# Gated products: the root-mean-square factors of four heads computed on four partitions and spread back by products

## The reference, cut to what matters

```python
def _hgrn_branch(q, v, f_fwd, f_bwd, og, norm_g, ...):
    ...
    o = (o_f + o_b[:, :, ::-1]).astype(jnp.float32)
    o = o * lax.rsqrt(jnp.mean(jnp.square(o), axis=-1, keepdims=True) + RMS_EPS)
    B, H, T, dh = o.shape
    o = (o.transpose(0, 2, 1, 3).reshape(B, T, H * dh) * norm_g).astype(q.dtype)
    return o * jax.nn.silu(og), s_f, s_b

def _merge(u_four, o_hgrn, gate_pre, w_fp, w_hp, w_o, b_o):
    g_four, g_hgrn = jnp.split(jax.nn.sigmoid(gate_pre...), N_BRANCHES, axis=-1)
    y = g_four * (_fourier_mix(u_four) @ w_fp) + g_hgrn * (o_hgrn @ w_hp)
    return y @ w_o + b_o
```

## Time and profile before

| | us |
|---|---|
| median of 3 runs | 3388.22 |
| lowest and highest | 3383.31, 3389.66 |
| span of the profiled execution | 3383.8 |
| of it, first to last instruction of the gated products | 1460.5 to 1726.8 |

### The profile page before, as it was taken

How to read it: one execution, slowest core, us unless ns; L and a number is a source line. 1 busy time by engine, 2 the same in 40 slices (tenths; PEclk the granted TensorE clock), 3 DMA queues, 4 the chain that set the end, 5 groups by cost and what they waited for, 6 DMA issues and landing times. The chain is left out here.

```text
span 3383.8 us, 35637 instructions
## 1 busy us (share of the span) xinstructions
PE 3140.5 (93%) x14552; PEld 2562.5 (76%) x14552; DVE 1852.5 (55%) x2585; ACT 615.2 (18%) x1048; POOL 301.3 (9%) x453
## 2 busy tenths in 40 slices
PE   5999999999996899929969999999999999999997
PEld 3878788888884688826758878888888778888886
DVE  3831133121222888657758775666655666666556
ACT  1421000111112556521001221111111101111110
POOL 0323011000001212200000000000000000000000
PEclk8999999999998999969989999999999999999999
DMA  6642233233235533345554721221114321111111
GB/s 216 208 138 78 75 101 124 103 122 115 96 107 165 150 109 111 99 158 193 173 172 148 226 77 48 63 69 63 56 48 126 122 69 58 58 60 60 50 44 62
DMA packets 261127, 365.32 MB, mean 108 GB/s; under 512 B 15443, under 2 KB 171363, under 8 KB 259430
## 3 DMA queue, kind: packets, MB, share of 16 engines
q1 hardware_dynamic: 203926, 197.33, 19.2%
q0 software_dynamic: 43680, 134.26, 11.4%
q10 hardware_dynamic: 13360, 31.46, 2.9%
HBM read 256.55 MB, written 106.44 MB: 107 GB/s over the span
## 5 line engine op out<-in xcount | busy, mean ns | idle before, releaser
L137 PE MATMUL head_bank<-head_hTh,head_wh 128*128 128x512 f32 x1024 | 407.2, 398 | 3.1 <-DVE head_hTl L549 2.3
L1971 PE MATMUL tail_bank<-tail_h2h,tail_w1h 128*128 128x512 f32 x1024 | 400.8, 391 | 4.5 <-DVE tail_w1l L1740 4.5
L139 PE MATMUL head_bank<-head_hTh,head_wl 128*128 128x512 f32 x1024 | 404.9, 395 | 0.0
L138 PE MATMUL head_bank<-head_hTl,head_wh 128*128 128x512 f32 x1024 | 404.9, 395 | 0.0
L1989 PE MATMUL tail_bank<-tail_w2h,tail_ah 128*128 128x512 f32 x1024 | 400.2, 391 | 4.0 <-DVE tail_acc L1770 4.0
L1972 PE MATMUL tail_bank<-tail_h2l,tail_w1h 128*128 128x512 f32 x1024 | 400.4, 391 | 0.0
L1973 PE MATMUL tail_bank<-tail_h2h,tail_w1l 128*128 128x512 f32 x1024 | 400.1, 391 | 0.0
L1990 PE MATMUL tail_bank<-tail_w2l,tail_ah 128*128 128x512 f32 x1024 | 399.8, 390 | 0.0
L1991 PE MATMUL tail_bank<-tail_w2h,tail_al 128*128 128x512 f32 x1024 | 399.8, 390 | 0.0
L557 DVE CAST head_wh<-head_raw 128x1024 fp32r<-128x1024 f32 x64 | 44.5, 695 | 583.5 <-PE head_bank L139 432.0
L1772 DVE TENSOR_TENSOR tail_acc<-tail_acc,tail_bank 128x512 f32<-128x512 f32 x416 | 275.6, 684 | 118.5 <-PE tail_bank L1991 116.4
(11 more groups left out here) (228 smaller groups left out, 4755.8 us busy)
## 6 DMA issues: line engine op xcount, KB each, us to landing
tail_raw<-in_w SPq DMA_DIRECT2D x128, 512.0 KB, 4.0
head_raw<-in_w_in SPq DMA_DIRECT2D x64, 512.0 KB, 4.1
scratch_proj<-head_stage POOLq DMA_DIRECT2D x128, 256.0 KB, 2.7
head_x<-in_w_ada ACTq DMA_DIRECT2D x8, 2048.0 KB, 10.1
merge_gates<-scratch_proj SPq DMA_DIRECT2D x32, 512.0 KB, 5.1
head_wa<-in_w_ada SPq DMA_DIRECT2D x8, 1024.0 KB, 5.3
mix_dec<-scratch_proj SPq DMA_DIRECT2D x32, 256.0 KB, 3.9
scratch_dft_a<-mix_fa POOLq DMA_DIRECT2D x32, 256.0 KB, 4.0
```

The costliest lines, as they stand in the source:

```text
L137: nc.tensor.matmul(out, wh, xh, start=(k == 0), stop=False)
L138: nc.tensor.matmul(out, wh, xl, start=False, stop=False)
L139: last = nc.tensor.matmul(out, wl, xh, start=False, stop=(k == k_tiles - 1))
L1971: nc.tensor.matmul(U[2 * e + c][:], w1h[:, e, k, :], hT[0][:, k, cs], start=(k == 0), stop=False)
```

## The change

The mean square is no longer spread over all partitions by its product. `sel[:, h, :]` is a weight tile of 128 x 4 whose column h is 1/128 and the rest zero; four products into the same bank, with `start` at the first and `stop` at the last, gather the four heads in rows 0 to 3 of one 4x512 tile. ScalarE takes one root of it (out `rr`), VectorE one reciprocal (`inverse`). Then `spread` multiplies `rr` with `back[:, h, :]`, a 4 x 128 tile that has ones in row h, and so puts head h's factor on all partitions of bank 7 (even h) or 6 (odd h). `part_c` multiplies straight from that bank.

The places in the queues change with it. VectorE: `inverse` in step 2, heads 0 and 1 in step 4, heads 2 and 3 in step 5, `part_d` in step 6. TensorE: heads 0 and 1 are spread after step 3, heads 2 and 3 after step 4; at the start the spreads stand behind the first and second `fourier` group.

```diff
+        sel, back = bx.sb("sel", [P, KB, KB]), bx.sb("back", [KB, KB, P])
+        rr = bx.sb("rr", [KB, 512])
+        sel_s, rc_s, br_s = bx.sem("sel_ready"), bx.sem("rms_inverse"), bx.sem("rms_spread")
...
+            def inverse(b):
+                dve.wait_ge(rt_s, b + 1)
+                if b:
+                    dve.wait_ge(br_s, KB * b)
+                nc.vector.reciprocal(rr[:], rr[:]).then_inc(rc_s, 1)
+
             def part_c(b, h):
 
-                dve.wait_ge(rt_s, KB * b + h + 1)
-                step.up(nc.vector.reciprocal(o2[:, 1, h], o2[:, 1, h]))
-                step.wait(dve)
-                nc.vector.scalar_tensor_tensor(sq[:, h], o2[:, 0, h], ng[:, h:h + 1], o2[:, 1, h], ALU.mult, ALU.mult
+                dve.wait_ge(br_s, KB * b + h + 1)
+                nc.vector.scalar_tensor_tensor(sq[:, h], o2[:, 0, h], ng[:, h:h + 1], bank[7 - h % 2][:], ALU.mult, ALU.mult
                                                ).then_inc(norm_s, 1)
...
+            step.up(nc.vector.memset(sel[:], 0.0))
+            step.wait(dve)
+            for h in range(KB):
+                nc.vector.memset(sel[:, h, h:h + 1], 1.0 / P)
+                last = nc.vector.tensor_copy(back[:, h, :], g["ident"][0:KB, h:h + 1].to_broadcast([KB, P]))
+            last.then_inc(sel_s, 1)
             part_a(0)
             weights(0, KB)
             part_b(0)
+            inverse(0)
...
-                    elif m < 5:
-                        for h in ((0, 1), (2,), (3,))[m - 2]:
+                    elif m == 2:
+                        inverse(b + 1)
+                    elif m in (4, 5):
+                        for h in ((0, 1), (2, 3))[m - 4]:
                             part_c(b + 1, h)
-                    elif m == 5:
+                    elif m == 6:
                         part_d(b + 1)
...
-                for h in range(KB):
-                    act.wait_ge(ms_s, KB * b + h + 1)
-                    nc.scalar.activation(o2[:, 1, h], bank[6 + h % 2][:], ACT.Sqrt, bias=g["eps"][:, 1:2]).then_inc(rt_s, 1)
+                act.wait_ge(ms_s, b + 1)
+                if b:
+                    act.wait_ge(br_s, KB * b)
+                nc.scalar.activation(rr[:], bank[6][0:KB, :], ACT.Sqrt, bias=g["eps"][0:KB, 1:2]).then_inc(rt_s, 1)
...
+                if b:
+                    pe.wait_ge(norm_s, KB * b)
+                else:
+                    pe.wait_ge(sel_s, 1)
                 pe.wait_ge(sq_s, b + 1)
                 for h in range(KB):
+                    last = nc.tensor.matmul(bank[6][0:KB, :], sel[:, h, :], sq[:, h], start=(h == 0), stop=(h == KB - 1))
+                last.then_inc(ms_s, 1)
+
+            def spread(b, heads):
+                for h in heads:
+                    pe.wait_ge(rc_s, b + 1)
                     if KB * b + h >= 2:
-                        pe.wait_ge(rt_s, KB * b + h - 1)
-                    nc.tensor.matmul(bank[6 + h % 2][:], g["mean"][:], sq[:, h], start=True, stop=True).then_inc(ms_s, 1)
+                        pe.wait_ge(norm_s, KB * b + h - 1)
+                    nc.tensor.matmul(bank[7 - h % 2][:], back[:, h, :], rr[:], start=True, stop=True).then_inc(br_s, 1)
...
             for m in range(3):
                 fourier(0, m)
+                if m < 2:
+                    spread(0, (2 * m, 2 * m + 1))
...
                     if m == 1 and b < NB - 1:
                         mean_square(b + 1)
+                    if m in (3, 4) and b < NB - 1:
+                        spread(b + 1, ((0, 1), (2, 3))[m - 3])
```

## The result

| | before | after |
|---|---|---|
| median of 4 runs, us | 3388.9 | 3419.1 |
| lowest and highest | 3383.3, 3390.3 | 3415.2, 3421.6 |
| span of the profiled execution | 3383.8 | 3413.3 |
| first sum-of-squares product to the end of block 3 | 251.6 | 281.0 |

The changed kernel is slower: ratio 1.0093, 95% interval 1.008 to 1.0106, some 30 us. The prediction had the sign; its 3400.5 us was 18.6 short, and the result lies above its range. The spans differ by 29.5 us and the stage by 29.4, so all of it is in the gated products.

A forecast was written before the change was run, and what follows sets the result against it. TensorE was taken to set the pace, waiting for VectorE at hand-overs. 6.3 us per hand-over, three times 18.9, minus 2.5 and 4.1 gave +12.3: span 3396.1, plus 4.4 to the median, 3400.5 us; range 3393 to 3413.

The forecast's parts named there:

- Reciprocal: VectorE, each block: one 4x512 reciprocal takes 3.34 us like each of the four wide ones, so VectorE loses 10.0 us.
- Selector products: TensorE's queue: four new spreading products per block cost full price, +3.33 us per hand-over.
- The first pair's wait: Spreads after step 3 wait for the inverse behind step 2's gating: 5.61 us against a step of 5.44, +0.17.
- The wait for head 0's bank: Spreads after step 4: TensorE idles until VectorE has gated and normalised head 0, +3.0 us per hand-over.
- Hand-over: Between blocks: operand preparation moves to step 6, so TensorE waits 2.71 us instead of 2.91, -0.20.
- Before the sums of squares: Blocks 1 and 2, step 0: VectorE is on time, the wait becomes 1.03 us, together 2.5 saved.
- Start: Start of the stage: VectorE is through earlier and weight loads shift along, -4.1 us, bounds -6.0 and -2.4.
- Clock: Three 1.2 GHz stretches expected behind waits for head 0, none behind hand-overs: 0 change, bounds -5.0 and +5.0.
- the one with more low clock (3412): Rival: low clock behind all six waits and sums of squares, with a worse start: +24, 3412 us; chance 0.18.
- The clock didn't stay high: Rival: no new wait is followed by 1.2 GHz and the start gains most: +5.4, 3393.6 us; chance 0.10.
- TensorE did wait: Opposite rival: at steps 4 to 6 and hand-overs TensorE doesn't wait, VectorE was the bound: -10.4, 3377.8 us; chance 0.03.
- narrow products were not free: Opposite rival: sums and spreads, 3.33 us each per block, cost nearly nothing: -7.7, 3380.5 us; chance 0.04.

The follow-up runs named there:

- one wait less: Changed kernel with heads 0 and 1 normalised in step 3 instead of step 4: 3400.5 us against 3387.8 before, ratio 1.0039.
- all waits moved: Changed kernel with heads 0 and 1 normalised in step 3, heads 2 and 3 in step 4, operand preparation in step 5: 3389.2 us, ratio 1.0004 to before.
- The best kernel found with it: Changed kernel with wide spreads, earlier inverse, normalisations and preparation, split start weights, `o` load in step 5: 3370.4 us against 3389.2 before, ratio 0.9949.
- the best found without it: Kernel before with two of four second-weight splits moved behind block 0's first normalisation: 3381.9 us, ratio 0.9976.
- best kernel narrow: The best kernel found with it, but spreads contracted over 4 partitions again: 3384.2 us against 3370.4 for the wide one, ratio 0.9987 to before.

## Why the prediction was right in direction and wrong in size

It said +12.3 us of span and had +29.5. The pieces:

- **Reciprocal: right.** The 4x512 reciprocal took 3.33 us (1604.76 in block 1), as the 128x512 one of the earlier trace rows. VectorE lost the 10 us per block.
- **Selector products: right.** The first pair's passes are 0.43 us apart (0.53 behind the first; 1.98 us recorded for four), so 3.43 us per block against 3.33 forecast. The Trainium skill's rule in TensorE: Matmul & The Clock Gate, section Why this matters for your kernels, that a product with few contraction rows takes as long as a full one, agrees with the trace at equal clock: 0.43 us with 4 rows, 0.42 with 128.
- **The first pair's wait: right**, small; together with the changes between kinds of product it is in the 1.5 us of rest. In block 1 it is 1607.79+0.23 to 1608.15, 0.13 us, with 0.17 forecast:

```profile
1607.79 0.39 PE L139 MATMUL merge_bank<-merge_oh,merge_wpl 128*128 128x512 f32 x1
1608.15 1.98 PE L1512 MATMUL merge_bank<-merge_rr,merge_back 4*128 4x512 f32 x4
```

- **The wait for head 0's bank: right**, 3.07 in each block against 3.0, with the chain as described.
- **Hand-over: right**, 2.72 against 2.71.
- **Before the sums of squares: right**, 1.12 twice against 1.03; saved 2.3 against 2.5.
- **Start: half right.** -2.4 instead of -4.1, at the bound given, but by luck: the bound's reason was low clock for the spreads, and the clock was back at 2.4 GHz when the first pair began (1494.24). Each pair, its short wait included, took 2.3 and 2.0 us to the next product and not 1.67, and the group between them 2.9 instead of 2.72. VectorE then multiplied at 1502.08 instead of the forecast 1500.1, 0.7 us of which is that the whole stage began later (1473.66 instead of 1472.92):

```profile
1502.08 2.29 DVE L1416 TENSOR_TENSOR merge_sq<-merge_sq,merge_og 128x2048 f32<-128x2048 f32 x1
...
1519.38 0.80 PE L137 MATMUL merge_bank<-merge_oh,merge_wph 128*128 128x512 f32 x1 [15.25 <-DVE merge_wpl L1440]
```

  The forecast had 1517.
- **Clock: wrong, and this is the step that failed.** The step took "2.43 had no consequence", set the hand-over's 2.55 beside it, and concluded that three low stretches would move from the hand-overs to the second pairs: 0 in sum, at most +5.0. Measured is +13.7: 3.4 us low behind each hand-over as before (its 2.56 was nearer to 2.75 than to 2.43 in effect), 6.8 behind each second pair, and 3.4 behind two of the three first pairs. In the terms of the step: the hand-overs' low clock, which was to go, stayed (3 x 1.7 = 5.1 us), and the narrow spreads added 3 x 1.7 at the second pairs and 2 x 1.7 at the first (8.5 us; with wide spreads exactly these five stretches were absent). The bound failed too, since it allowed one stretch of 3.4 us per wait and none without a wait. What it lacked is the effect of the narrow products themselves, which no row of before could show, and it leaned on a single wait of 2.43.

In the sum: clock 13.7, start 1.7, changes between kinds of product about 1.0, small differences in waits and passes 0.7 make 17.1 of the 17.2 us between forecast (3396.1) and profile. The 4.4 us added between span and median are 5.8 after (3419.1-3413.3), which is the remaining 1.4 of the 18.6.

Of the rivals, the one with more low clock (3412) came nearest, for a part of its reason: all hand-overs and second pairs, but not the sums of squares of blocks 1 and 2, and with a length that it did not have. The clock didn't stay high, TensorE did wait, narrow products were not free, and the reciprocal freed VectorE; those four fell. What was said to show it held except for two lines: blocks 1 and 2 of 59 us were 64.8, by 10.2 us more at 1.2 GHz (5.1) and 0.7 of rest, and the first `oh` product was 2.4 us late, 0.7 of it the later start of the stage.

The price of the order and that of the width are apart now: against the changed kernel, one wait less is worth 17 us, all waits moved 29, wide spreads alone 11. What is left of the change as an idea is -21 for the reciprocals against some 10 of products. The best kernel found with it is 11 us faster than the best found without it (-19 against -8 beside their own runs of before), but it needed wide spreads, another order and an earlier load for that.

## What to carry to other kernels

Before work is moved from VectorE to TensorE, ask which engine sets the pace: here VectorE got 10 us per block, TensorE paid 3.4, and VectorE's time was worth money only at the hand-over, at the start and, by about 2 us, before the sums of squares. A product that waits for a bank must not be queued right behind the step whose result the reader of that bank handles first; one step of distance was worth 17 us. And a small product in the middle of a stream of large ones is better written over all 128 partitions with zero rows, if memory allows: here a pair took no longer (1.31 us instead of 1.91), and the clock did not fall behind it.

## What the runs showed of the hardware

- **Narrow contractions and the granted clock.** Pairs of spreads in the blocks with no wait over 1.6 us ahead of them: with 4 contraction rows the clock fell to 1.2 GHz for about 3.4 us within 3.4 us of the pair's start behind 9 of 21 (after 2 of 3, heads 0 and 1 early 3 of 6, all early 1 of 6, best kernel narrow 3 of 6); with 128 rows, of which 124 were zero, behind none of 27 (wide spreads 3, and 6 in each of four kernels). Behind a wait of 3.07 us it was low for 6.8 us with narrow and 3.4 with wide ones, three times each. TensorE was recorded busy all the while. Why 9 pairs and not the other 12 stays open, and widths between 4 and 128 rows were not tried. Sums of squares with 128 contraction rows and weights of 4 columns did nothing of the kind: none of 11 behind a wait of 1.12 us was followed by 1.2 GHz.
- **Waits and the granted clock.** TensorE's idle times at the hand-overs, 2.56 to 2.77 us as the rows give them, were in 18 of 18 cases (three in each of six kernels) followed by 1.2 GHz, which began during the wait or within 1.5 us behind it; the 0.96 before the sums of squares never were. Between them both are seen: 1.92 and 2.17 were followed by it, 1.59, 1.88 and the 1.79 and 2.43 of the earlier trace rows weren't. So 2.43 was a single case, and no line can be drawn from it.
- **Changes between kinds of product.** A float32 pair between rounded products took 1.31 us (wide, 1580.58 to 1581.89) and 1.91 (narrow, 1603.74 to 1605.65) from its start to that of the next product. The Trainium skill, TensorEngine Tiling (Array Packing), Key Properties, says that a change of tiling mode drains TensorE. A drain would fit where most of the 0.6 us stand, behind the last pass (0.52 us to the next product's start instead of 0.03), and the sums of squares show the same 0.52 with weights of 4 columns and 0.03 with 128; but nothing here shows that a drain is the cause.

```profile
1580.58 1.88 PE L1513 MATMUL merge_bank<-merge_rr,merge_back 128*128 128x512 f32 x4
1581.89 0.80 PE L137 MATMUL merge_bank<-merge_fh,merge_wfh 128*128 128x512 f32 x1
```

- **A load's place in the queue.** Asking for the two 1024 KB loads of `o` in step 5 instead of 7 took some 13 us off one kernel (3384.0 to 3370.4; -6 to -19 beside their own runs of before) and added 11 to another (3381.9 to 3393.0). The two kernels differ in much, among it when the buffer of `o` comes free: 1539.5 in the first and 1555.9 in the second, in block 0.
